# When ScalarE empties the output bank of a stick-breaking attention layer, and when it issues that output's stores

## What is computed

```python
x = x + mixer_stick_breaking(rmsnorm(x, a_norm[0]), a_w_in[0], a_w_out[0])
return rmsnorm(x, final_norm)

def mixer_stick_breaking(h, w_in, w_out):
    q, k, v, g = jnp.split(jnp.einsum('bsd,de->bse', h, w_in), 4, axis=-1)
    o = stick_breaking_attention(q, k, v)            # per head
    return jnp.einsum('bse,ed->bsd', o * jax.nn.silu(g), w_out)

# stick_breaking_attention, t0 a block of 128 queries, s < t only:
z = einsum(q[t0:t0+128], k[:t0+128]) * scale
w = exp(log_sigmoid(z) + sum over s < j < t of log_sigmoid(-z[t, j]))
out = w @ v
```

## Time and profile before

| | |
|---|---|
| median of 3 runs | 1701.12 us (1698.07 to 1701.83) |
| profiled execution | 1702.32 us, its span 1700.6 us |
| TensorE's granted clock over the span | 0.989 |
| busy: TensorE, VectorE, ScalarE, GpSimd | 94%, 76%, 50%, 25% of the span |
| stretch 242 to 1439 us (slots 0 to 149) | TensorE busy 1126 of 1197 us, VectorE 999 |
| stretch 1439 to 1531 us (slots 150 to 159) | TensorE busy 83 of 92 us |
| behind it | the output projection alone, to 1700.6 us |

### The profile page before, as it was taken

One profiled execution on the slowest core, in us unless ns is written; L12 is line 12 of the kernel. 1 busy time (PEld: TensorE's weight loads), 2 busy tenths in 40 slices (PEclk: granted clock), 3 DMA queues, 4 the chain that ended last, 5 costly groups with the idle time before them and its releaser, 6 DMA issues.

```text
span 1700.6 us, 34166 instructions
## 1 busy us (share of the span) xinstructions
PE 1603.1 (94%) x13762; PEld 1394.9 (82%) x13762; DVE 1288.6 (76%) x1525; ACT 849.0 (50%) x1558; POOL 425.1 (25%) x520
## 2 busy tenths in 40 slices
PE   9999989898999999999999999999999998899998
PEld 7888878787888888888888888888888887778887
DVE  5536248697888888887888888888888887776874
ACT  6635235455555555555555555455555555643221
POOL 0022033133352234123422342144314322000000
PEclk9999989999999999999999999999999999999999
DMA  8959543343434242424333342434242435569722
GB/s 297 280 177 288 154 137 105 102 122 94 120 99 122 75 138 80 131 77 142 93 113 113 111 117 85 126 92 134 71 134 88 134 92 164 199 204 354 241 106 82
DMA packets 214076, 237.80 MB, mean 140 GB/s; under 512 B 54560, under 2 KB 170272, under 8 KB 213920
## 3 DMA queue, kind: packets, MB, share of 16 engines
q1 hardware_dynamic: 121536, 160.30, 30.5%
q10 hardware_dynamic: 92384, 75.33, 14.8%
HBM read 155.78 MB, written 79.76 MB: 139 GB/s over the span
## 4 chain that ended last, share of the span: by engine, by line
PE 80%; ACT 6%; DMA 5%; ACTq 4%; issue 1%; DVE 1%; POOL 1%; SPq 1%; DVEq 0%
PE z_ps L820 30%; PE z_ps L833 11%; PE o_ps L885 7%; PE o_ps L884 7%; PE turn_ps L867 5%; PE z_ps L773 5%; PE turn_ps L915 5%; PE z_ps L915 4%; PE o_ps L773 3%; PE turn_ps L773 3%; ACT u L1070 2%; ACTq L1088 2%; ACT o_stage L1081 2%; ACTq L1087 2%; DMA gate_cols<-made_lo 2%; DMA qk_lo_cols<-made_lo 1%
## 5 line engine op out<-in xcount | busy, mean ns | idle before, releaser
L1288 DVE TENSOR_TENSOR_SCAN u<-u,u 128x512 f32<-128x512 f32 x384 | 499.3, 1336 | 0.0
L820 PE MATMUL z_ps<-hT_hi,w_hi 128*128 128x256 f32 x1536 | 455.4, 296 | 2.4 <-DVE made_lo L1274 1.5
L1070 ACT ACTIVATE u<-z_ps 128x512 f32<-128x512 f32 (+3 forms) x640 | 311.5, 550 | 275.4 <-PE z_ps L833 258.2
L1292 DVE TENSOR_TENSOR r_turned_lo<-turn_ps,r_turned_hi 128x1024 fp32r<-128x1024 f32 (+1 forms) x320 | 325.0, 1057 | 160.9 <-ACT r_turned_hi L1075 160.2
L820 PE MATMUL z_ps<-hT_hi,w_lo 128*128 128x256 f32 x1536 | 437.3, 285 | 0.0
L820 PE MATMUL z_ps<-hT_lo,w_hi 128*128 128x256 f32 x1536 | 437.3, 285 | 0.0
L820 PEld LDWEIGHTS z_ps<-hT_hi,w_hi 128*128 128x128 f32 x1536 | 296.7, 193 | 48.8 <-issue 36.6
L820 PEld LDWEIGHTS z_ps<-hT_lo,w_hi 128*128 128x128 f32 x1536 | 297.6, 194 | 0.0
L820 PEld LDWEIGHTS z_ps<-hT_hi,w_lo 128*128 128x128 f32 x1536 | 297.0, 193 | 0.0
L1075 ACT ACTIVATE r_turned_hi<-turn_ps 128x1024 fp32r<-128x1024 f32 (+1 forms) x320 | 270.7, 909 | 7.4 <-issue 3.8
L833 PE MATMUL z_ps<-k_hi_twice,q_hi 64*128 64x512 f32 (+3 forms) x640 | 158.2, 461 | 86.0 <-ACT u L1070 65.1
(11 more groups left out here) (140 smaller groups left out, 2079.1 us busy)
## 6 DMA issues: line engine op xcount, KB each, us to landing
qk_hi_cols<-made_hi ACTq DMA_DIRECT2D x128, 128.0 KB, 2.4
qk_lo_cols<-made_lo ACTq DMA_DIRECT2D x128, 128.0 KB, 2.3
k_hi_twice<-qk_hi_cols SPq DMA_DIRECT2D x128, 128.0 KB, 3.1
k_lo_twice<-qk_lo_cols SPq DMA_DIRECT2D x128, 128.0 KB, 3.5
x_T<-in_xT SPq DMA_DIRECT2D x29, 512.0 KB, 6.2
w_raw<-in_w_qkg SPq DMA_DIRECT2D x24, 512.0 KB, 3.8
x_rows<-in_x SPq DMA_DIRECT2D x16, 512.0 KB, 5.3
v_rows<-v_stage ACTq DMA_DIRECT2D x32, 256.0 KB
```

The source lines that it names most:

```text
L820: last = nc.tensor.matmul(bank_of(g)[:, 0:GW], a[t % 2][:, k, :], b[:, c // 2, k, cols], start=(n == 0), stop=(n == QPM - 1))
L1070: nc.scalar.activation(u_t[(m // CB) % RU][r][:, 0:w], z_ps[r % 3][:, 0:w], ACT.Sigmoid, scale=-Z_SCALE).then_inc(s_u, 1)
L1288: nc.vector.tensor_tensor_scan(u, u, other, start, ALU.mult, op).then_inc(s_r, 1)
L1292: nc.vector.tensor_tensor(by_halves(rt_lo[p % 2][:], p), turned(p), by_halves(as_f32(rt_hi[p % 2][:]), p), ALU.subtract).then_inc(s_lo, 1)
```

## The change

The output bank's copy moves from the head of a chunk-end slot to behind the unit's two high parts, and the two stores move behind the second pair of sigmoids. Nothing is added or removed.

```diff
                 for s in range(-LEAD, LAST_SLOT + 1):
                     ended = chunk_end(s - 1) if inside(s - 1) else None
-                    if ended is not None:
-                        empty(ended)
-                        store_o(ended)
                     if inside(s + LEAD):
                         stick(CB * (s + LEAD))
                         stick(CB * (s + LEAD) + 1)
@@
                     if inside(s):
                         hi(2 * s)
                         hi(2 * s + 1)
+                    if ended is not None:
+                        empty(ended)
                     if inside(s + LEAD):
                         stick(CB * (s + LEAD) + 2)
                         stick(CB * (s + LEAD) + 3)
+                    if ended is not None:
+                        store_o(ended)
                     for m in range(CB * s, CB * s + CB):
                         if m in HI_W:
                             weight_hi(HI_W[m])
```

## The result

The changed kernel takes 1640.53 us (median of 4 runs, 1635.69 to 1641.57), against 1699.59 us for the kernel before in the same rounds. The ratio is 0.9646, 95% interval 0.9622 to 0.967: 3.5% faster. The medians differ by 59.1 us, the means of the runs by 60.2. The profiled execution took 1639.75 us, its span is 1638.0 us, 62.6 less than before, and TensorE's granted clock is 0.993.

A forecast was written before the change was run, and what follows sets the result against it. TensorE, 94% busy, was taken as the bound, waiting 62.6 us for sigmoids, mostly queued behind ScalarE's copy and store issues. 52.2 + 5.4 - 1 - 0.9 - 2 = 53.7 us gain; forecast 1647.5 us, range 1640 to 1661.

The forecast's parts named there:

- The mechanism: In chunk-end slots copy and store issues no longer delay the first sigmoid TensorE awaits; 1640 to 1661 us, chance 0.83.
- something else: Three chunk-end slots after 1439 us, where TensorE waits at the slot's head for another cause; no gain counted.
- surplus of long stalls: Waits for the first sigmoid longer than 0.96 us in the 58 chunk-end slots; their excess recovered, 5.4 us.
- all 61.1 us with no loss: Best end of the main case's range: every sigmoid wait of the 58 chunk-end slots recovered, 1640 us.
- 58 x 0.90: 58 chunk-end slots each gain 0.90 us between first and second scores; 52.2 us.
- Slot 17: ScalarE waits there for GpSimd, whose chain gets no faster, so the slot's gain is lost; 0.9 us charged.
- VectorE's carry: VectorE carries about 0.4 us from slots like 54 into the next, which has 0.7 to spare; cost 0, narrowly.
- a sign of being wrong: Slots 55, 65, 75 getting longer by what slots 54, 64, 74 lose would count against the forecast.
- The 1 us for collisions: Charge for the whole run, covering colliding store issues along with VectorE's lateness; 1 us.
- The tail: Last chunk's empty waits for the previous chunk's later-issued stores to land in the one staging tile; 2 us charged.
- VectorE as the bound: Rival: VectorE carries more, so the 16 slots like 54 give nothing, gain 40.1 us; 1661 us, chance 0.12.
- The bank free too late: Rival: the later empty ends after TensorE is ready to weight the new chunk; slower, 1712 us, chance 0.03.

The follow-up runs named there:

- first experiment: Against the changed kernel, the copy goes back to the slot's head and only the stores stay behind the second sigmoids; 1641.01 us.
- stall experiment: The changed kernel with 3, 7, 11 or 15 dummy activations ahead of the first sigmoid of eight slots; 1667.05 us.

## Where the prediction was right, and the step that failed

**The step that failed.** The mechanism held, and a term was mis-sized. The sum gave slots 148 to 156 a gain of 0.9 us, slot 149's, and put the other chunk ends there at nothing, as slots "in which TensorE waits for something else at the slot's head". They gained 6.2 us in the profiled pair: that "something else" was the landing of the gate's store, and the change moved the transfers that held it up. The second mis-sized term is the surplus of long stalls, priced at their idle time and without the half clock behind them. Both are taken up below. That the time still fell inside the range, 0.5 us from its end, is partly luck: the range's best case was "all 61.1 us with no loss", while in fact losses of some 2 us came true and were outweighed by gains that no term held.

**What bounds the kernel, and the mechanism: right.** The 62.6 us of waits for line 1070 fell to 1.1, first to second scores fell from 2.54 to 1.64 us, the copy stands 3.03 us after the head, and no wait for the bank appeared. The prediction took copy and issues together (1.73 us); the first experiment shows that the issues alone were the delay.

**58 x 0.90: right.** Of the 58 chunk-end slots before slot 148, 43 gained between 0.7 and 1.0 us, 37.9 us in all, 0.88 each. Of the other 15, ten gained 1.10 to 3.68 us, most of them long stalls, and five less than 0.7: slots 17 and 47, which the prediction set apart, and 27, 74 and 124 (0.58 to 0.67), which it did not. The reason given for 0.90, other widths, was not tested.

**The surplus of long stalls, 5.4 us: too small.** Most were recovered at their length (slot 129: wait 2.36, gain 2.30; slots 50 and 70: 1.52 and 1.47, gains 1.47 and 1.40). But slots 4 and 9 had waits of 1.81 and 2.25 us and gained 3.14 and 3.68. The windows of the kernel before, filtered to PE (busy, granted clock, DMA share, GB/s), show what lay behind them:

```profile
277.70:281.10 3.40, 3.40 (x16) 0.50 0.29 79
318.60:322.00 3.40, 3.40 (x19) 0.50 0.00 0
```

The prediction priced a stall at its idle time; here the change also removed 3.4 us at 1.2 GHz behind it. The stall experiment made such stretches on purpose, and they cost 1.3 to 2.2 us beyond the stall. It is not so behind every stall. From slot 0 on, the profiles of before and of the two kernels that keep most of the old order have 5, 8 and 8 waits for a sigmoid of over 1.3 us; 5 of these 21 were followed by half clock within 2 us, 2, 2 and 1 in turn. So this term is real, varies between executions, and was 3.14 + 3.68 - 1.81 - 2.25 = 2.8 us in the profiled one. From slot 0's head to slot 157's the granted clock was half for 23.9 us before and for 10.2 us in each of the three profiles of the changed kernel; but the kernel with the new order only from slot 147 on had 6.8 us, so the difference cannot all be put down to the edit.

**Slots 148 to 156: 0.9 us forecast.** The prediction set the chunk ends behind slot 149 aside as "three slots after 1439 us in which TensorE waits for something else at the slot's head". Slots 148 to 156 gained 6.2 us (5.3 and 4.3 in the two other profiles of the changed kernel), of which slot 149 2.13, slot 150 2.49 and slot 154 0.98. The kernel before, too, is one profile: the one with the new order in the first slots only takes 83.95 us here instead of 86.62, against which the three gain 1.6 to 3.5. The "something else" was a landing of the gate's store, and the change moved the chunk's two stores from in front of it to behind it. The section on what the change moves asked which queued work passes the stores on ScalarE, but counted only engine time, not the transfers that no longer stand ahead of line 1052's. For slot 149 the cause is shown, by the experiment with the chunk's stores in front and by the one with the stores alone. Slot 150's gain is half clock that did not come, 6.83 us of it, behind a wait for the same landing that had become 1.41 us instead of 2.66; which shorter wait is followed by half clock is not settled. Slot 154's gain is mostly the wait at the next slot's head, 0.61 us instead of 1.46, again for VectorE's low part; that one was not tested by itself.

**The charges.** Slot 17: 0.9 charged; it gained 0.55 instead of about 0.9, so 0.35 was lost. VectorE's carry was priced at nothing and cost some tenths of a microsecond in a few slots. Slots 54 and 55 of the changed kernel (heads at 657.00 and 663.89) on DVE and PE, answering to the earlier trace rows:

```profile
660.71 1.52 DVE L1293 TENSOR_TENSOR r_turned_lo<-turn_ps,r_turned_hi 128x896 fp32r<-128x896 f32 x2
...
667.21 2.32 DVE L1293 TENSOR_TENSOR r_turned_lo<-turn_ps,r_turned_hi 128x1024 fp32r<-128x1024 f32 x2
...
669.14 0.40 PE L884 MATMUL o_ps<-r_turned_hi,dv_head 128*128 128x512 f32 x1
...
670.07 0.39 PE L884 MATMUL o_ps<-r_turned_hi,dv_head 128*128 128x512 f32 x1
```

VectorE ends the low parts at 669.53. TensorE weights with the first of them from 669.14 on and needs the second at 670.07, 0.54 us later; no wait is named, and slot 55 is as long as before. Here the carry stays within what the slot could bear. But slots 75, 95 and 125, each behind such a slot, are 0.13, 0.34 and 0.13 us longer, and TensorE waits for VectorE's made_lo, 0.15 us before slot 75's head, which is about what slot 74 gained less than others of its kind, and 0.34 before slot 96's. Slots 75 and 125 take 7.33 or 7.34 us in all ten profiles with the new order there and 7.21 in the three with the old, so this small cost belongs to the change. It is a sign of being wrong that the prediction named, at a small size. The 1 us for collisions can be neither shown nor ruled out: in slots 0 to 147 those that are no chunk ends lost 1.2 us together, the 0.6 of these three among them, and slots 25 (0.65 longer) and 48 (1.48 longer) against 11 and 46 (0.91 and 0.72 shorter) also differ between profiles of the same kernel. Slot 11's wait, which was to stay, is gone in this profile and back in the second (1.22 us). The tail: 2 charged, 1.3 measured, released by a landing as forecast. With the last two chunks in the old order it is as long as before (192.86 against 192.89), so the landing that SyncE awaits before group 0's last part cost nothing.

**The rivals.** VectorE as the bound: no, though line 884 now waits once for line 1293 (0.48 us in slot 152, which is no longer than before). The bank free too late: no wait for it in any profile. The rule of the Trainium skill weighed against this edit ("PSUM — Partial Sum Buffer", summary of rules for kernel authors, to evacuate promptly) cost nothing here: the kernel with the copy at the slot's head and the one with it 3 us later are within 0.5 us. The other rule of the Trainium skill, in "Perfetto Trace Analysis" (HWDGE DMA instruction), agrees with the row of 0.86 us for line 1088 in slot 57, an issue 0.25 us longer than the same one before, with SyncE's issue of line 546 begun 0.01 us ahead of it; the loss that the rule allowed did not come, as no urgent work is queued behind it. In the kernel with both moves behind the high parts the same 0.86 us stand ahead of two sigmoids and count.

## What to carry to other kernels

A store's issue took its engine's queue 0.45 to 0.61 us here, at times up to 1.74; put it behind whatever another engine waits for, and leave cheap compute in idle time where it is. When a store is moved, ask not only who is queued behind its issue but which other transfers share the queues with its data, before and behind it: a landing that someone awaits came 2.1 us earlier here, twice what the two issues cost. And price a stall of two or three microseconds in a nearly full TensorE above its length: the half clock that can follow it cost 1.2 to 2.2 us more. Last, a single profile of a kernel whose long stalls wander is one draw; by one profile slots 4 and 9 gained some 2 us more each than by the other.

## What was not expected of the hardware

- In the stall experiment the granted clock of TensorE fell to half (1.2 GHz) for 3.41 or 6.83 us behind waits of 1.55 to 3.85 us, in most cases after the engine had worked again for 0.2 to 1.8 us, once (3.85 us) before the wait had ended; not behind 0.41 us. Behind other waits of 1.3 to 2.4 us it happened in some and not in others of the same length (2.25 yes, 2.36 no).
- A store issued 1.5 us earlier, relative to the slot's head, let its tile go no earlier (7.90 against 7.75 us after the head); one issued 1.1 us later and behind two others let it go 2.1 us later. And stores issued behind it can hold it up: with the two chunk stores 1.66 us behind it instead of 2.76, it landed 7.8 us after its issue instead of 6.6, the first of them before it.
- Kernels that differ only behind slot 159 had medians of 1643.01 and 1640.55 us, over 5 and 6 runs; the tail is 1.3 us shorter, so it should have been the other way round. The one profile has two more stretches of half clock in slots whose order is the same. Whether these come from the edit is not settled.
